# Gate one-hots of a PEER layer: one VectorE compare for four tokens, the gate factor put on by ScalarE, a ring of four

## What is computed

```python
# q: 8 heads x 2 x 128; sub_keys: 2 x 128 x 128
v1, i1 = top_k(s1, 16); v2, i2 = top_k(s2, 16)        # per head
top_score, top_pos = top_k(v1[:, None] + v2[None, :], 16)
expert_idx = i1 * 128 + i2                             # of the 16 chosen pairs
gate = softmax(top_score)
# per token: 8 heads x 16 = 128 chosen experts
act = gelu(expert_u[expert_idx] @ h) * gate
out = act @ expert_v[expert_idx]
```

## Time and profile before

| | us |
|---|---|
| median of 3 runs (lowest, highest) | 2983.47 (2969.54, 2986.14) |
| the profiled execution, its own time | 2975.43 |
| its span | 2973.7 |
| TensorE busy in the span | 2803.9 (94%) |
| VectorE busy | 2233.4 (75%) |
| ScalarE busy | 1181.3 (40%) |
| GpSimd busy | 1533.8 (52%) |

### The profile page before, as it was taken

The page is one execution under the profiler, slowest core; times in us unless marked ns, Lnnn a source line. Parts: engine busy times, 40 slices in busy tenths (PEclk is TensorE's granted clock), DMA queues, the critical chain, the costliest instruction groups (busy, mean ns, idle before and its releaser), DMA issues.

```text
span 2973.7 us, 43212 instructions
## 1 busy us (share of the span) xinstructions
PE 2803.9 (94%) x17757; PEld 2643.4 (89%) x17757; DVE 2233.4 (75%) x3157; ACT 1181.3 (40%) x1387; POOL 1533.8 (52%) x664
## 2 busy tenths in 40 slices
PE   7899899988999989989999899999999999999998
PEld 6677788866879989989999899999999999999997
DVE  6756576766677789979997577777777777778786
ACT  6755532357323333333433333434333333333321
POOL 0000154222242367863334488888867777766662
PEclk9999999989999999999999899999999999999999
DMA  9737638863797868877789899999999999999995
GB/s 362 277 142 263 232 128 328 335 255 127 301 355 279 341 247 297 298 276 298 309 304 371 333 371 353 379 366 383 376 360 407 411 411 388 393 384 382 364 371 217
DMA packets 189485, 949.46 MB, mean 319 GB/s; under 512 B 18352, under 2 KB 77792, under 8 KB 79552
## 3 DMA queue, kind: packets, MB, share of 16 engines
q1 hardware_dynamic: 116704, 485.55, 43.5%
q0 software_dynamic: 60848, 440.59, 38.0%
q10 hardware_dynamic: 11808, 21.70, 1.9%
HBM read 906.46 MB, written 41.22 MB: 319 GB/s over the span
## 4 chain that ended last, share of the span: by engine, by line
PE 69%; DVE 11%; DMA 11%; ACT 5%; POOL 2%; issue 1%; SPq 1%; ACTq 0%; DVEq 0%
PE ps L1686 14%; PE ps L2034 8%; PE ps L2036 8%; PE ps L2035 8%; PE ps L1967 7%; PE ps L1965 6%; PE ps L1966 6%; PE ps L1950 4%; DVE ring_lo L1099 4%; PE ps L1673 4%; DMA ring_raw<-peer_v 3%; POOL ring_lo L617 2%; DVE ps L1341 2%; ACT ring_hi L689 2%; DVE hot_a L1535 2%
## 5 line engine op out<-in xcount | busy, mean ns | idle before, releaser
L617 POOL TENSOR_TENSOR ring_lo<-ring_raw,ring_hi 128x2048 fp32r<-128x2048 f32 x215 | 1000.1, 4652 | 701.5 <-ACT ring_hi L689 699.9
L689 ACT ACTIVATE ring_hi<-ring_raw 128x2048 fp32r<-128x2048 f32 x400 | 762.0, 1918 | 688.2 <-DMA ring_raw<-peer_u 222.8
L1965 PE MATMUL ps<-bT_hi,ring_hi 128*128 128x304 f32 x2048 | 629.3, 307 | 33.0 <-DVE ring_lo L1099 24.8
L2034 PE MATMUL ps<-a_hi,ring_hi 128*128 128x304 f32 x2048 | 629.3, 307 | 31.2 <-DVE ring_lo L1099 15.8
L2036 PE MATMUL ps<-a_hi,ring_lo 128*128 128x304 f32 x2048 | 624.7, 305 | 0.0
L1967 PE MATMUL ps<-bT_hi,ring_lo 128*128 128x304 f32 x2048 | 624.2, 305 | 0.0
L1966 PE MATMUL ps<-bT_lo,ring_hi 128*128 128x304 f32 x2048 | 623.3, 304 | 0.0
L2035 PE MATMUL ps<-a_lo,ring_hi 128*128 128x304 f32 x2048 | 621.8, 304 | 0.0
L1099 DVE TENSOR_TENSOR ring_lo<-ring_raw,ring_hi 128x2048 fp32r<-128x2048 f32 x185 | 452.6, 2462 | 174.9 <-ACT ring_hi L689 174.7
L1965 PEld LDWEIGHTS ps<-bT_hi,ring_hi 128*128 128x128 f32 x2048 | 392.5, 192 | 35.3 <-issue 30.2
L2034 PEld LDWEIGHTS ps<-a_hi,ring_hi 128*128 128x128 f32 x2048 | 390.8, 191 | 36.8 <-issue 27.2
(11 more groups left out here) (310 smaller groups left out, 3772.3 us busy)
## 6 DMA issues: line engine op xcount, KB each, us to landing
ring_raw<-peer_u SPq DMA_DIRECT2D x128, 1024.0 KB, 7.6
ring_raw<-peer_v SPq DMA_DIRECT2D x128, 1024.0 KB, 8.0
ring_raw<-w_in SPq DMA_DIRECT2D x80, 1024.0 KB, 5.4
ring_raw<-w_out SPq DMA_DIRECT2D x32, 1024.0 KB, 4.8
ring_raw<-w_query SPq DMA_DIRECT2D x32, 1024.0 KB, 6.5
g_pair<-gates_scratch SPq DMA_DIRECT2D x64, 320.0 KB, 8.8
gelu_scratch<-ahead ACTq DMA_DIRECT2D x72, 152.0 KB, 5.3
g_in<-gelu_scratch SPq DMA_DIRECT2D x72, 152.0 KB, 7.5
```

The lines of the kernel that those rows point to most:

```text
L617: pool.tensor_tensor(ring_lo[s][:], ring_raw[s][:], ring_hi[s][:].bitcast(F32), ALU.subtract)\
L689: act.activation(ring_hi[place(n)][:], ring_raw[place(n)][:], ACT.Copy).then_inc(hi_ok[SLOT[n]], 1)
L1965: pe.matmul(dst, hi[:, e], bT_hi[:, k, 0:NEAR], start=(k == 0), stop=False)
L2034: pe.matmul(dst, hi[:, col], a_hi[:, par, e, :], start=(e == 0), stop=False)
```

## The change

Both one-hots of a group's four tokens are made by one `tensor_tensor` compare of 1024 columns on VectorE. The gate factor, which the four `tensor_scalar` instructions multiplied in, is now put on by ScalarE: four activations (Copy with a scale from a column of `selT`) of 128 columns, in place, for each group, queued before the copy of the group two earlier. The ring of one-hot buffers grows from three groups to four; VectorE's lead over TensorE is two groups in place of three, and in a hot tile the row is taken between its second and third group in place of behind the fourth. TensorE waits for the scaled one-hots. Two semaphores of the attention part are merged into one to make room for the new one.

```diff
-HOT_RING = 3
+HOT_RING = 4
+HOT_LEAD = 2
...
-    hot_a = at("hot_a", [P, 4 * HOT_RING, NK], F32, 144)
-    hot_b = at("hot_b", [P, 4 * HOT_RING, NK], F32, 150)
+    hots = [at(f"hots_{r}", [P, 2, 4, NK], F32, kb) for r, kb in enumerate((144, 148, 152, 188))]
...
+            def scales_upto(count):
+                while scaled[0] < min(count, N_HOT):
+                    j = scaled[0]
+                    scaled[0] += 1
+                    act.wait_ge(hot_made, j + 1)
+                    for q in range(4):
+                        one = hots[j % HOT_RING][:, 0, q, :]
+                        last = act.activation(one, one, ACT.Copy, scale=selT[:, 2, 4 * j + q:4 * j + q + 1])
+                    last.then_inc(hot_scaled, 1)
...
                 for _ in range(HOT_AT[i]):
+                    scales_upto(jj + HOT_LEAD + 1)
                     copy_gates(jj)
...
-                first, tok = 4 * (jj % HOT_RING), 4 * jj
-                for q in range(4):
-                    dve.tensor_scalar(hot_a[:, first + q, :], iota[:], selT[:, 0, tok + q:tok + q + 1],
-                                      selT[:, 2, tok + q:tok + q + 1], ALU.is_equal, ALU.mult)
-                dve.tensor_tensor(hot_b[:, first:first + 4, :], bcast(iota[:], [P, 4, NK], 1),
-                                  bcast(selT[:, 1, tok:tok + 4], [P, 4, NK], 2), ALU.is_equal).then_inc(hot_made, 1)
+                tok = 4 * jj
+                shape = [P, 2, 4, NK]
+                dve.tensor_tensor(hots[jj % HOT_RING][:], iota[:].unsqueeze(1).unsqueeze(1).broadcast_to(shape),
+                                  bcast(selT[:, 0:2, tok:tok + 4], shape, 3), ALU.is_equal).then_inc(hot_made, 1)
...
-                    hots_upto(used + HOT_RING)
-                    rows_step(ROWS_AT[AHEAD + i])
+                    left = ROWS_AT[AHEAD + i]
+                    for q in range(HOT_AT[i]):
+                        hots_upto(used - HOT_AT[i] + q + 1 + HOT_LEAD)
+                        if q == 1 and left:
+                            rows_step(1)
+                            left -= 1
+                    rows_step(left)
                     lo_upto(AHEAD + i + 2)
...
-                pe.wait_ge(hot_made, j + 1)
+                pe.wait_ge(hot_scaled, j + 1)
```

More of the change, by code:

```diff
@@ L336, in layer @@
         qk_a, qkT_a, qkT_a_out = sem("qk_a_normed"), sem("qk_a_turned"), sem("qk_a_copied")
-        z_a, z_a_ln, sp_zb_a, tails_a, w_a, pv_a, y_a = (sem("z_a"), sem("z_a_ln"), sem("sp_a_then_z_a_blocked"),
-                                                        sem("tails_a"), sem("w_a"), sem("pv_a"), sem("y_a"))
+        z_pv_a, z_a_ln, sp_zb_a, tails_a, w_a, y_a = (sem("z_a_then_pv_a"), sem("z_a_ln"), sem("sp_a_then_z_a_blocked"),
+                                                     sem("tails_a"), sem("w_a"), sem("y_a"))
         s_sgm, vb_a, mix_a, gated_a = sem("gmlp_a_masked"), sem("vb_a"), sem("mix_a"), sem("gated_a")
@@ L364, in layer @@
         ahead_stored = [sem(f"ahead_stored_{b}") for b in range(2)]
-        hot_made, g_mm, g_out, g_stored = sem("hot_made"), sem("g_mm"), sem("g_out"), sem("g_stored")
+        hot_made, hot_scaled, g_mm, g_out, g_stored = (sem("hot_made"), sem("hot_scaled"), sem("g_mm"), sem("g_out"),
+                                                       sem("g_stored"))
         g_loaded = [sem(f"gates_loaded_{q}") for q in range(2)]
@@ L782, in _ @@
                     zA = ps[:, 2:4, :].rearrange("p b (h n) -> p (b h) n", h=4)
-                    act.wait_ge(z_a, 1)
+                    act.wait_ge(z_pv_a, 1)
                     act.activation(sptA[:], zA, ACT.Abs).then_inc(z_a_ln, 1)
@@ L794, in _ @@
                 elif i == 8:
-                    act.wait_ge(pv_a, 1)
+                    act.wait_ge(z_pv_a, 2)
                     act.activation(qA[:], ps[:, 5:7, :].rearrange("p b n -> p (b n)"), ACT.Copy).then_inc(y_a, 1)
@@ L1022, in copy_gates @@
                    .then_inc(g_out, 1)
+            scaled = [0]
+            def scales_upto(count):
[7 more added lines that the diff above has]
+                    last.then_inc(hot_scaled, 1)
             def gelu_to_psum(i, bank):
@@ L1736, in _ @@
                                          start=(h % 4 == 0), stop=True, skip_group_check=True)
-                    last.then_inc(z_a, 1)
+                    last.then_inc(z_pv_a, 1)
                 elif i == 7:
@@ L1748, in _ @@
                                          vA[:, h * HD:(h + 1) * HD], start=True, stop=True)
-                    last.then_inc(pv_a, 1)
+                    last.then_inc(z_pv_a, 1)
                     pe.wait_ge(y_a, 1)
@@ L2006, in outers @@
                 for q in range(4):
-                    m = 4 * (j % HOT_RING) + q
-                    last = pe.matmul(ps[:, j % 2, q * NK:(q + 1) * NK], hot_b[:, m, :], hot_a[:, m, :],
+                    a, b = hots[j % HOT_RING][:, 0, q, :], hots[j % HOT_RING][:, 1, q, :]
+                    last = pe.matmul(ps[:, j % 2, q * NK:(q + 1) * NK], b, a,
                                      start=True, stop=True)
```

## The result

The changed kernel takes **2990.03 us** in the median (2979.03 to 3010.65, 20 runs), the kernel before beside it 2983.93 us (2969.54 to 2988.74, 20 runs): a ratio of **1.0033**, with a 95% interval of 1.0017 to 1.005. So the change costs 0.2 to 0.5%, some 5 to 15 us. The profiled execution of the changed kernel (3010.65 us, span 3008.6) is 20 us above its own median. A second profile of the same kernel (experiment 10) has a span of 2981.2 us; of the 27.4 us between the two, 8.0 lie ahead of the first group and 19.1 behind the last, where nothing was changed. So only the hot stretch is compared here: from the start of the first group to the start of the last it takes 284.5 us before, 292.5 after and 292.2 in the second profile, 8 us longer.

The account below looks back on a forecast made before the run. TensorE (56.8) and VectorE (56.2 of 61.4 us a batch) nearly tie, with TensorE waiting for `ring_lo`. Profiled 2975.4 + 1.6 = 2977.0, plus 8.0 to the median: 2985 us; own bounds -6 and +13 us; range 2953 to 3002; chance 0.62 for within 0.5%.

Parts of the forecast that it names:

- a wait that moves from tile 6 to tile 1': TensorE's wait in each of four passages moves to the next batch's first tile and keeps its size: +1.6 us in all.
- The wait for `ring_lo` goes, all four times: TensorE's wait at tile 6 vanishes, since `ring_lo` ends before GpSimd's subtraction; 7.0 us a batch could be had, 29 in all.
- Compare: VectorE's one compare of 1024 columns a group: 1216 ns, 1.14 us with overlap, in place of 1.63 us.
- The rival of the halved pace: Broadcast operands halve the compare's pace on VectorE: 2.2 us a group, 44 us slower, 3029 us; chance 0.02.
- Scaling: ScalarE's four scaled copies a group take 1.0 us, bounds 1.0 and 1.66; room for 1.3, so no cost in hot tiles.
- ScalarE becomes the bound: Rival: at 0.414 us a scaled copy, ScalarE exceeds its room in hot tiles by 26 us in all, 3011 us; chance 0.12.
- What is late next, r8: The last gathered row before tile 1' one-hots lands at T+20.5, T being the end of tile 4's work on TensorE.
- The load of tile 3': The load that ScalarE's `ring_hi` awaits lands at T+22.0, letting TensorE's third group of tile 1' start at T+25.5.
- r8's chain: From r8 at T+20.5: row 2.27, compare 1.14, scaling 1.0 and 0.2 give TensorE's third group at T+25.1.
- The clock: TensorE's stand of 5.4 us before the third group lowers its clock level, costing 2.3 us more a passage.
- The batch: Third group at T+27.8 in effect against T+27.1, less 0.3: +0.4 us a batch, +1.6 us for four.
- The rush clears in time: Rival: load and r8 land by about T+16.5 and T+15.5, TensorE never stands: 2954 us; chance 0.24 for over 0.5% faster.

Follow-up runs that it names:

- experiment 10: The changed kernel measured again with no edit, beside the kernel before: 2992.33 us, ratio 1.0043.
- experiment 4: The changed kernel with only its order edits: old one-hots back on VectorE, no scaling on ScalarE; 2990.93 us, ratio 1.0029 to the kernel before.
- experiment 5: The changed kernel with only the new compare and scaling; ring of three, lead and row place as before the change; 2976.94 us, ratio 0.9987.
- experiments 7: The changed kernel with one row moved from tile 6 to tile 1, ScalarE's copies before `ring_hi`, VectorE three groups ahead; 2965.38 us, ratio 0.9948.
- experiment 8: The kernel of experiments 7 with the old one-hots, all on VectorE, and no scaling on ScalarE; 2983.08 us, ratio 1.0008 to the kernel before.
- experiment 9: The kernel of experiments 7 with rows per tile (2, 2, 1, 1, 1, 1) in place of (2, 1, 1, 1, 2, 1); 2949.03 us, ratio 0.9896.
- experiment 3: The changed kernel with each store of the gate matrices cut to an eighth, loads unchanged in number and size; 2959.38 us, ratio 0.9913.
- experiments 6: The changed kernel with one row moved from tile 6 to tile 1 and ScalarE's copies before `ring_hi` in hot tiles; 2970.38 us, ratio 0.9957.

## Why the prediction was right, and where it was off

The predicted 2985 us was 5 below the median of 2990, and "within 0.5%" holds. The mechanism was the forecast one, a wait that moves from tile 6 to tile 1' behind the late transfers; its size was not: +1.6 us was forecast and +10.4 measured. The number is near because both are small beside 15 us, not because the sum was right.

- **The wait for `ring_lo` goes, all four times:** so it was. The prediction gave this to the new place of `ring_lo`; experiment 4 shows that this is enough, and experiment 5 that the compute part is enough without it.
- **Compare:** 1216 ns forecast, 1220 measured in the median, 1.14 from one to the next. The mean in the row, 1279, holds one at the start of the stretch that took 5.6 us. The rival of the halved pace is out.
- **Scaling:** 1.0 us a group was too low. Four copies take 1.17 us until the next instruction starts (1341.09 to 1342.26 in a hot tile), 0.29 each, 390 ns singly. The Trainium skill, "ScalarE: Activation LUTs", section "What ACT_TABLE_LOAD costs", gives 186 ns and 0.833 ns a column with 93 for the pointer scale, 386 in all, and 0.29 with the overlap; this case agrees for a source in SBUF. The sixteen copies from PSUM, which I took for the like, are 0.25 apart: nearest was not near enough. It stayed below the 1.3 of room, and groups of a hot tile remain 2.55 us apart, so the rival "ScalarE becomes the bound" is out: its price would have been 26 us. The Trainium skill's same page, section "Rules for kernel authors", sends multiplications to VectorE. Here, with VectorE late, the kernel that has the factor on ScalarE is 12.5 us of whole faster (experiments 7 and 8); but the two differ in the merged compare as well, which the move made possible, and no run separates them.
- **What is late next, r8:** T+20.5 was forecast, T+22.0, 23.4, 22.4 and 22.0 was measured (VectorE's first row behind its wait, 1390.02, 1455.35, 1519.50 and 1583.58, less T). I had credited 3.2 us for a gather that left the rush and a faster issue; the issue did fall from 2.82 to 0.95 us, but against the 23.7 of before only 0.3 to 1.7 came. **This is the mis-sized term.** The load of tile 3' came at T+22.0, 20.0, 19.7 and 20.9 against T+22.0 forecast. So r8's chain was the later one, not the load's.
- **A missed link in r8's chain:** I ended it with 1.0 for the scaling and 0.2. But ScalarE scales group 3' and then copies group 1', in this order, and TensorE's third group needs the copy. In the first passage the chain is 22.0 + 2.26 + 1.25 + 1.19 + 0.57 + 0.14 = T+27.4, as measured; with r8 at 23.4, 22.4 and 22.0 the same sum gives the other three, 28.8, 27.8 and 27.4. Forecast was T+25.1: 1.5 of the difference are r8, 0.6 the copy, 0.2 the scaling.
- **The clock:** 2.3 us more a passage, as forecast and as before.
- **The batch:** +0.4 forecast. The mean third group is T+27.85, so 27.85 + 2.3 - 27.1 - 0.3 = +2.75; measured, from the first T to the last group, +11.5 over four passages, +2.9. Against that stands a gain of 1.0 us from the transposition to the first T (58.1 in place of 59.1), which the prediction had at nothing. So +10.4 in place of +1.6; the bound with r8 and the load as before had said +13.
- **"The rush clears in time"** did not happen by the change. Its price of 29 us below the kernel before was about right: experiment 9 takes 23.5 of it by order (31 by the ratio, 24 to 38) and experiment 3 16.6 by smaller stores (26 by the ratio, 17 to 35). Where the differences between whole and ratio come from isn't shown; behind the last group single executions differ by up to 32 us.
- **"A batch again near 61 us"** was wrong by three to four (63.9 to 65.1); the four waits forecast at 4 to 7 us were 7.2 to 8.6.

Open: why r8 and the stores of `gbuf` come when they do within a passage (r8 at T+22.0 to 23.4, the first copy behind the stores at T+18.1 to 23.0 in experiments 6, 7 and 9); experiment 3 shows that the amount of stores decides most of it, and no run takes the rest apart.

## What to carry to other kernels

When an engine in program order waits for a transfer, what counts is not how long it waits but what stands behind it in its queue: move the instruction that needs the late transfer behind those that the bounding engine needs soon, on each queue at once, since two chains that end within a few microseconds of each other hide each other's removal. Shortening the lead of a producer showed no cost inside the hot tiles here (groups stayed 2.55 us apart), and all of it at the four places where transfers come in a burst; look for such places. Measure a stretch from a point ahead of the first instruction that the change can delay: counted from the first group, this change seemed to cost 8 us in place of 10.4. And follow a chain link by link through every engine's written order, the instructions in between included.

## What the runs showed that was not expected

- A gather issued at the same time (T+9.0, first passage) takes 5.9 us to land with an eighth of the stores and 13.0 with all of them. The stores are thus more than half of its time.
- Issuing a gather took GpSimd 0.95 us while VectorE stood idle and 2.82 beside VectorE's `ring_lo`.
- Short compares are held up beside GpSimd's subtraction just as VectorE's own 2048-column subtraction is: four of 128 columns took 5.34 us in place of 1.10 (experiment 8), one of 1024 columns in experiment 9 took 3.65 in place of 1.22. It works in the other direction too: in the bad passage of experiment 8 GpSimd's own next subtraction took 6.90 us in place of 4.6. VectorE's timeline of experiment 9, then GpSimd's of experiment 8:

```profile
1429.13 3.65 DVE L1552 TENSOR_TENSOR hots<-iota,selT 128x1024 f32<-128x1024 f32 x1
```

```profile
1430.98 6.90 POOL L618 TENSOR_TENSOR ring_lo<-ring_raw,ring_hi 128x2048 fp32r<-128x2048 f32 x1
```

- Scaled copies of 128 columns ran 0.29 us apart from SBUF in the changed kernel and 0.25 from PSUM in the kernel before.
